# Products of a constant table in TensorE's waits, in a two-block transformer kernel

## What is computed

```python
def first_block(x, c, ...):
    for l in range(2):
        x = hybrid_layer(x, c, ...)      # neighbourhood, latent and grouped attention, gated feed-forward
    return rms_norm(x, final_norm_g)

def second_block(x, ...):
    # w_in gives four branches: a gated linear recurrence with a convolution, a chunked gated delta rule
    # (chunks of 64), stick-breaking attention, chunked gated linear attention (chunks of 16);
    # four gates merge them, w_out, layer norm, then a mixture of experts:
    # 16 experts in 4 groups, a router picks one group and 2 experts in it, D_EXPERT = 512; layer norm
```

## Time and profile before

| | |
|---|---|
| median of 3 runs | 1780.77 us (1774.51 to 1784.77) |
| the profiled execution | 1777.7 us, of which the span of its instructions is 1775.8 us |
| busy, share of the span | TensorE 89%, weight loads 81%, VectorE 69%, ScalarE 46%, GpSimd 2% |
| mean granted clock of TensorE | 0.954 of the higher level |

### The profile page before, as it was taken

The page is one execution under the profiler, slowest core; times in us unless marked ns, Lnnn a source line. Parts: engine busy times, 40 slices in busy tenths (PEclk is TensorE's granted clock), DMA queues, the critical chain, the costliest instruction groups (busy, mean ns, idle before and its releaser), DMA issues. The chain is left out here.

```text
span 1775.8 us, 25493 instructions
## 1 busy us (share of the span) xinstructions
PE 1587.9 (89%) x10701; PEld 1438.4 (81%) x10701; DVE 1223.5 (69%) x1352; ACT 818.2 (46%) x952; POOL 43.7 (2%) x60
## 2 busy tenths in 40 slices
PE   2799998899989999899979999787689979999995
PEld 2789988899878988899969898686678777888884
DVE  4877577788766648756555784633566868899895
ACT  1345544334334554444433465223453346777774
POOL 0100000000010000000000000000000000000000
PEclk9999999999999999999989999897898989999998
DMA  8974444999855323566626563111222437999993
GB/s 308 315 239 138 162 135 140 345 328 323 297 150 166 118 97 125 198 212 214 225 75 191 157 190 119 53 44 48 72 95 72 157 130 254 372 361 370 367 355 124
DMA packets 226056, 348.05 MB, mean 196 GB/s; under 512 B 14612, under 2 KB 156672, under 8 KB 225808
## 3 DMA queue, kind: packets, MB, share of 16 engines
q1 hardware_dynamic: 225936, 346.36, 58.2%
HBM read 345.29 MB, written 1.97 MB: 196 GB/s over the span
## 5 line engine op out<-in xcount | busy, mean ns | idle before, releaser
L465 PE MATMUL bank<-layer_split,hT_pair 128*128 128x256 f32 (+2 forms) x4032 | 515.0, 288 | 30.4 <-DVE hT_pair L1042 20.8
L465 PEld LDWEIGHTS bank<-layer_split,hT_pair 128*128 128x128 f32 x4032 | 488.4, 191 | 44.5 <-issue 28.6
L188 DVE TENSOR_TENSOR layer_split<-layer_raw,layer_split 128x2048 fp32r<-128x2048 f32 x122 | 279.6, 2292 | 104.5 <-ACT layer_split L176 103.0
L176 ACT ACTIVATE layer_split<-layer_raw 128x2048 fp32r<-128x2048 f32 x122 | 233.6, 1915 | 198.0 <-PE bank L465 76.1
L188 DVE TENSOR_TENSOR expert_split<-expert_raw,expert_split 128x2048 fp32r<-128x2048 f32 x96 | 219.0, 2288 | 26.4 <-ACT expert_split L176 25.9
L176 ACT ACTIVATE expert_split<-expert_raw 128x2048 fp32r<-128x2048 f32 x96 | 183.4, 1917 | 55.8 <-PE bank L2490 31.5
L465 PE MATMUL bank<-split_w,hT_pair 128*128 128x256 f32 (+1 forms) x1248 | 169.7, 296 | 9.5 <-ACT mixer_arena L2797 3.4
L465 PEld LDWEIGHTS bank<-split_w,hT_pair 128*128 128x128 f32 x1248 | 158.6, 195 | 20.1 <-issue 11.5
L1911 PE MATMUL bank<-layer_split,ffnh_aT 128*128 128x512 f32 x528 | 127.0, 396 | 2.8 <-DVE ffnh_aT L1983 2.8
L465 PE MATMUL bank<-hT_pair,split_w 128*128 128x256 f32 x960 | 119.5, 285 | 2.4 <-DVE hT_pair L321 1.7
L465 PEld LDWEIGHTS bank<-hT_pair,split_w 128*128 128x128 f32 x960 | 116.9, 192 | 4.3 <-issue 2.9
(11 more groups left out here) (468 smaller groups left out, 1944.9 us busy)
## 6 DMA issues: line engine op xcount, KB each, us to landing
layer_raw<-in_ada_w SPq DMA_DIRECT2D x48, 1024.0 KB, 6.7
layer_raw<-in_ffn_w_gate_up SPq DMA_DIRECT2D x44, 1024.0 KB, 5.7
layer_raw<-in_w_in SPq DMA_DIRECT2D x38, 1024.0 KB, 6.4
expert_raw<-in_w_gate SPq DMA_DIRECT2D x32, 1024.0 KB, 7.5
expert_raw<-in_w_up SPq DMA_DIRECT2D x32, 1024.0 KB, 7.5
expert_raw<-in_w_down SPq DMA_DIRECT2D x32, 1024.0 KB, 7.3
raw_w<-in_w_in SPq DMA_DIRECT2D x30, 1024.0 KB, 5.4
layer_raw<-in_ffn_w_down SPq DMA_DIRECT2D x22, 1024.0 KB, 5.6
```

What stands on the lines that cost most here:

```text
L176: self.nc.scalar.activation(self.pair[:, j % self.pairs, 0, 0:self.size[n]], self.raw[n % self.depth][:, 0:self.size[n]], ACT.Copy).then_i ...
L188: self.nc.vector.tensor_tensor(self.pair[:, j % self.pairs, 1, 0:self.size[n]], self.raw[n % self.depth][:, 0:self.size[n]], self.pair[:, ...
L465: ins = nc.tensor.matmul(out, lhs, rhs, start=first and c == chunks[0] and tp + wp == 0, stop=last and c == chunks[-1] and tp == 1)
```

## The change

A helper, `keep_busy(bank, n)`, issues `n` products of the constant table with itself (128 rows, 128 columns; `ident` is the table's first part) into a bank that nobody reads at that time. Calls stand ahead of 24 waits on TensorE's queue, with 4 to 33 products each, and ahead of the four waits between the router's first score products, with one each. Where the bank is one of the ring of output banks, TensorE first waits until its former content has been read: by `self.jobs[-6].left` behind the first projection, `merged[-8].left` behind the merge, `Beside.keep_busy` in the recurrences, and `out.sem` in stick-breaking attention's last pair. In `small_products` the 256-column products move between the two tiles' 8-column products. Nothing else changes. The diff, cut where the same call is repeated with another number (the runs left out: 4, 8 and 4 in the two recurrences, 4 ahead of the last sums of gated attention):

```diff
+        def keep_busy(bank, n):
+            for _ in range(n):
+                nc.tensor.matmul(ps[bank][:, 0:P], ident, cst[:, 0:P], start=True, stop=True)
...
             def tensor(self, pe):                                   # Norm
+                keep_busy(3, 14)
                 for t in range(TILES):
                     pe.wait_ge(self.normed.sem, t + 1)
                     self.turn.tensor_tile(t)
+                keep_busy(3, 12)
...
+            def keep_busy(self, pe, n):                             # Beside
+                g = self.issued
+                if g >= len(self.banks):
+                    pe.wait_ge(*self.jobs[g - len(self.banks)].left)
+                keep_busy(self.banks[g % len(self.banks)], n)
...
                     ada.reduce(pe, 1)                               # Projection, first layer
+                    keep_busy(3, 32)
                     pe.wait_ge(ring.acc_left, ada.done_pe)
                 else:
+                    keep_busy(2, 13)
                     norm.turn(pe, 0)
+                    keep_busy(2, 8)
...
+                if self.l == 0:                                     # behind its jobs
+                    pe.wait_ge(*self.jobs[-6].left)
+                    keep_busy(len(self.jobs) % 6, 7)
...
                 down(blocks - 1)                                    # FeedForward
+                if self.norm_next is None:
+                    keep_busy(2, 12)
...
             def tensor(pe):                                         # routing
+                keep_busy(7, 25)
...
                             b = k // 2
+                            keep_busy(7, 1)
                             pe.wait_ge(dve_out if b % 2 else act_out, b // 2 + 1)
...
+                keep_busy(7, 6)
                 pe.wait_ge(member_out.sem, 1)
...
                     route_tensor(pe)
+                    keep_busy(7, 10)
                     pe.wait_ge(g_ready, 1)
...
                     for t in range(TILES):                          # small_products
                         for c in range(KD):
-                            nc.tensor.matmul(ps[7][:, 8 * t:8 * t + 8], hT[:, c, t * P:(t + 1) * P], small[:, c, 0:8],
+                            ins = nc.tensor.matmul(ps[7][:, 8 * t:8 * t + 8], hT[:, c, t * P:(t + 1) * P], small[:, c, 0:8],
+                                                   start=c == 0, stop=c == KD - 1)
+                        for c in range(KD if t == 0 else 0):
+                            nc.tensor.matmul(ps[7][0:16, S:2 * S], small[:, c, 8:24], hT[:, c, :],
                                              start=c == 0, stop=c == KD - 1)
-                    for c in range(KD):
-                        ins = nc.tensor.matmul(ps[7][0:16, S:2 * S], small[:, c, 8:24], hT[:, c, :],
-                                               start=c == 0, stop=c == KD - 1)
...
+                def after_merge(pe):
+                    pe.wait_ge(*merged[-8].left)
+                    keep_busy(len(merged) % 8, 6)
...
+                    beside.keep_busy(pe, 11)                        # lru_and_gdn
                     pe.wait_ge(attn.sem, 2)
...
+                            beside.keep_busy(pe, 31)
                             pe.wait_ge(started.sem, 4)
...
+                    beside.keep_busy(pe, 7)
                     pe.wait_ge(squared.sem, 3)
                     pe.wait_ge(u_out.sem, 2)
                     for b in range(2):
                         nc.tensor.matmul(ps[b][:, :], ones, half(W(SQ), b), start=True, stop=True).then_inc(n_sum, 1)
+                    beside.keep_busy(pe, 14)
...
                             n = i - 1                               # stick_breaking
+                            if n >= 3:
+                                pe.wait_ge(out.sem, n - 2)
+                            keep_busy(4 + i % 2, (10, 11, 11, 33)[n])
                             pe.wait_ge(kept.sem, 3 * n + 3)
...
-                for _ in range(5):                                  # gla
-                    yield
+                for i in range(5):
+                    if i == 3:
+                        keep_busy(4, 11)
+                    yield
+                keep_busy(4, 11)
                 pe.wait_ge(qk_ready.sem, 3)
```

More of the change, by code:

```diff
@@ L2922, in mixer @@
                 jobs = [job for n in range(1, 4) for job in merge_jobs(n, split.wait(n))]
-                project("mixer_merge", ring, jobs, norm=split)
+                merged = jobs
+                def after_merge(pe):
+                    pe.wait_ge(*merged[-8].left)
+                    keep_busy(len(merged) % 8, 6)
+                project("mixer_merge", ring, jobs, norm=split, extra={"tensor": after_merge})
                 jobs = []
@@ L3066, in tensor @@
                         yield
+                    beside.keep_busy(pe, 4)
                     pe.wait_ge(u_ready.sem, 10)
@@ L3070, in tensor @@
                     yield
+                    beside.keep_busy(pe, 8)
                     pe.wait_ge(keyed.sem, 4)
```

## The result

| | before | after |
|---|---|---|
| median of 10 executions each, same chip | 1781.89 us (1774.51 to 1788.34) | 1770.92 us (1763.47 to 1776.58) |
| ratio, 95% interval | | 0.9935 (0.9913 to 0.9958) |
| the profiled execution, and its span | 1777.7 us, 1775.8 us | 1771.72 us, 1770.0 us |
| mean granted clock | 0.954 | 0.974 |

The change makes the kernel 11 us faster (0.65%; the interval is 7.5 to 15.5 us).

What follows compares the result with a forecast made beforehand. TensorE was taken to run at half clock behind waits, binding only where no other engine sets the pace. Place gains summed to 20.3 us, less 1.8 for stretches staying slow: 18.5 us off the 1780.77 median, 1762 us, range 1749 to 1774.

Steps and rivals of the forecast that it cites:

- The bound, and the price of a run: All filled waits: an added product costs 0.23 us at the higher level, hidden by the wait, except three singles.
- Delta rule, stick-breaking, gather: Places ending a chain: delta rule 1.8, 1.8 and 1.9 us, stick-breaking 0.5 and 2.5, gather 2.2.
- The last sums: Delta rule's end: 4 products of 512 columns fall from 3.78 us to 4 x 0.46, gaining 1.9 us.
- the first three pairs: Stick-breaking: faster products gain 0 there, since ScalarE is busy with the next pair's logarithm; the pair's period stays.
- router and gather: Router gains 0, its faster transposes offset by three singles; the gather's 14 products could gain 3.1 us, 2.2 taken.
- The small products: Reordered small products: 16 of 256 columns fall from 5.31 to 3.7 us, gaining 1.6 us.
- First and second layer: Behind the first layer's projection 2.9 us, half of 5.78 at half clock; second layer's projection 1.3 us.
- Rival 2: Whole kernel: most of the gain is hidden, only first layer, small products and delta rule's sums pay; 8 us, 1773; chance 0.17.
- Rival 3: Ten waits: added products don't raise the clock, cost 0.47 us each and outlast waits; 26.6 us slower, 1807; chance 0.05.
- Rival 1: Behind the filled waits: all 80.15 us of work is on the path, half is 40 us, giving 1741; chance 0.09.
- The transposes: Output projection and gated attention's start: transposes share in the clock; otherwise some 2 us less gain.
- the forecast's own case: Whole kernel: time between 1750 and 1771 us, given a chance of 0.69.

Runs made afterwards that it cites:

- runs_in_recurrences: Kernel with only the added runs inside the delta rule, stick-breaking and gated attention, none elsewhere; 1768.30 us, ratio 0.9955 to before.
- fuller runs: After with the second table issued earlier and 21 products before the first layer's feed-forward transposes, each run lengthened by its wait's remainder; 1760.20 us, ratio 0.9893 to before.
- sixteen_columns: After with the same number of added products in the same places, each with 16 columns instead of 128; 1794.38 us, ratio 1.0092 to before.

## Why the prediction was right, point by point

**The bound, and the price of a run.** Right: 0.229 us a product, runs that end before the releaser (the exceptions found in after are the two runs that met the lower level, after which the products began 0.6 and 0.4 us late), and real products at the higher level behind them. No wait took the place of a removed one in attention, feed-forward or experts.

**Delta rule, stick-breaking, gather.** The mechanism is right, and the sizes are as near as the draws can tell. The last sums gave 1.8 for 1.9 and stick-breaking 3.2 for 3.0, with draws that agree to 0.3 us. That the first three pairs are worth nothing, the rows of before (the first two) and after show:

```profile
1223.76 1.23 PE L3406 MATMUL bank<-sb_gla_inputs 64*128 64x256 f32 x4 [5.76 <-PEq L3670]
1243.03 0.84 ACT L3478 ACTIVATE mixer_arena<-mixer_arena 128x768 f32<-128x768 f32 x1
1217.41 1.23 PE L3444 MATMUL bank<-sb_gla_inputs 64*128 64x256 f32 x4 [2.64 <-PEq L3715]
1232.40 1.02 DVE L3490 TENSOR_TENSOR mixer_arena<-mixer_arena,bank 128x384 f32<-128x384 f32 x2
1236.68 0.84 ACT L3519 ACTIVATE mixer_arena<-mixer_arena 128x768 f32<-128x768 f32 x1
```

Counted from the first scores, VectorE adds the first pair's sums at 16.62 us in before and at 14.99 in after, yet ScalarE's exp comes at 19.27 in both, and the last pair's L3417 at 55.13 in both (1278.89, 1272.54): ScalarE sets the pace. All of the 2.7 us that after won lies behind that L3417, where 2.5 were forecast. The 3.4 for 3.6 in the delta rule and the 2.4 for 2.2 in router and gather agree less well than they look: their two draws without runs lie 1.9 and 2.4 us apart, so agreement to 0.2 us is luck. Before and after alone differ there by 2.9 and 2.3. These were the steps with a row of the same instructions at both levels, and with a chain behind them that goes on at once.

**The small products: the step that failed.** "With the wide ones in the middle, 16 x 0.23 = 3.7 us: 1.6" has the right cost and the wrong end. I looked at what TensorE's next instruction waits for and not at the other queues that the block's end joins. The row was in the trace of before: SP had issued the table 7.8 us ahead of the block's end and waited 6.7 us for it. With the low clock that came behind it, a forecast gain of 1.6 became a loss of about 1.

**First and second layer: mis-sized.** Forecast 2.9 and 1.3, measured 1.6 and 0.6. I halved all the work done at the lower level in one profiled execution, as if each execution had that stretch and none came up elsewhere. after still has 3.41 us of low clock in attention at 107.42, and a new stretch at 554.56 us, where 24 products took 4.59 us behind a wait of 2.00 and had taken 2.98 behind the same wait in before; runs_in_recurrences, without a run there, began attention at the higher level (1.10 us for what took 2.04 in before). With one profile a kernel, how often each comes stays open.

**Rival 2** says "mostly hidden, 1773", and the measured 1770.92 lies between it and the forecast. But its list of what pays isn't the one that the stages show: the small products, which it counts, lost, and the first layer gave about half, while stick-breaking, which it leaves out, gave 3.2 us. Whether the empty end of the waits took a part stays open: what fuller runs brought can't be told from nothing. **Rival 3** didn't come about, and sixteen_columns shows where it would: at 0.43 us a product. It is in part there, though, whenever a run meets the lower level, as in the router, where five of ten profiles with the runs took 28.0 us or more (28.7 and 31.1 without).

**Rival 1, and a rule weighed.** The granted clock in the profiles is low for 150.15 us in before and 78.49 in after, and TensorE's work in those stretches fell by 29.5 us, half of which is 14.7. The Trainium skill, TensorE: Matmul & The Clock Gate, Terms, takes the penalty as half of the throttled time; by it the change would have given 36 us. The measured 11 us disagree: half of the busy time comes closer, and what lies beside other engines comes off that.

**The transposes.** Eight of the router's transposes took 1.09 us in after behind their run; sixteen at the lower level had taken 3.75, 1.9 for eight. The Trainium skill, the same page, Part 4, says that the higher level doesn't engage for transposes. No run here bears that out.

**The base.** The forecast was summed from one profiled execution, 4.2 us below the median of ten. In its gated attention the outputs took 39.9 us, which no later profile came near but one (sixteen_columns, 40.0). A sum of stages from one draw carries that draw's luck; I had put the width of the range on unknown costs alone, and the 10 us by which three executions of one kernel differ were in the table before I began. That 1770.92 falls 0.1 us inside the forecast's own case (1750 to 1771) is luck too: after's ten executions lie between 1763 and 1777.

## What to carry to other kernels

Filling a wait paid here where the product behind it is the last thing on the path, and not where another engine sets the pace: ask at each place who else joins there (a block's end joins SP's transfers too). Fill with wide products (128 columns ran at the higher level here, 16 in the same places at the lower), and remember that a run fitted at the higher level takes up to twice as long when it is met by the lower one, so leave room where the wait follows narrow work. Where the same code shows its low stretches in other places from one execution to the next, judge a change by the length of stages over several profiles, not by two.

## What had not been expected of the hardware

- Products of 16 columns, back to back with no idle time, stayed at the lower level for 13.24 us (62 instructions, 0.21 us each, granted clock 0.50), in the same place where 128-column ones ran at 0.114 us each.
- The same gate work, 24 products of 256 columns, took 2.97 to 5.49 us in gated attention, according to where the clock fell in that execution. The stage's length went from 39.9 to 48.6 us in kernels that differ in it by no more than the run of 4 and two moved jobs. That this is much of the 13 us between executions of one kernel is likely, but not shown, since each kernel has one profile; what decides it in a given execution is left open.
